# Two column groups of an output projection by Strassen: all sixteen row tiles in the seven products

## The reference

```python
h = rms_norm(x, norm_g)                            # x: 1 x 1024 x 2048, float32
proj = jnp.einsum('bsd,de->bse', h, w_in)
...                                                # attention of heads A, B and C
mixed = jnp.concatenate([
    out_a.astype(h.dtype) * jax.nn.silu(az),
    out_b.astype(h.dtype) * jax.nn.silu(bz),
    out_c.astype(h.dtype) * jax.nn.silu(cz)], axis=-1)
return x + jnp.einsum('bse,ed->bsd', mixed, w_out) # w_out: 2048 x 2048
```

## Time and profile before

| | |
|---|---|
| time, median of 3 runs | 2041.82 us (2039.94 to 2045.06) |
| the profiled execution's own time | 2044.43 us |
| its span | 2042.7 us |
| PE busy over the span | 98% |
| DVE, ACT, POOL busy | 55%, 44%, 25% |
| from 1985 to 2018 us: PE, DVE, POOL busy of 33 us | 32.85, 33.00, 30.01 |
| granted PE clock of that stretch | 1.00 of full speed (2.4 GHz) |

### The profile page before, as it was taken

One profiled execution on the slowest core, in us unless ns is written; L12 is line 12 of the kernel. 1 busy time (PEld: TensorE's weight loads), 2 busy tenths in 40 slices (PEclk: granted clock), 3 DMA queues, 4 the chain that ended last, 5 costly groups with the idle time before them and its releaser, 6 DMA issues.

```text
span 2042.7 us, 28729 instructions
## 1 busy us (share of the span) xinstructions
PE 2008.2 (98%) x10024; PEld 1690.6 (83%) x10024; DVE 1121.9 (55%) x1733; ACT 891.1 (44%) x1504; POOL 503.1 (25%) x400
## 2 busy tenths in 40 slices
PE   6999999999999999999999999999999999999998
PEld 5788888888888888888888888888888887788787
DVE  7611456465445555555555555555555657613797
ACT  7311343444454445445454445445444556411242
POOL 0000343251531212222221212222122210002565
PEclk9999999999999999999999999999999999999999
DMA  7322424324332222222222222323232274466646
GB/s 236 81 72 71 116 68 109 100 82 103 94 98 78 61 85 78 87 67 72 87 72 85 64 89 79 107 58 98 83 97 71 85 249 145 134 200 222 237 155 196
DMA packets 204559, 223.20 MB, mean 109 GB/s; under 512 B 17336, under 2 KB 143336, under 8 KB 203328
## 3 DMA queue, kind: packets, MB, share of 16 engines
q1 hardware_dynamic: 187760, 191.73, 31.8%
q10 hardware_dynamic: 16720, 30.45, 4.0%
HBM read 173.35 MB, written 48.78 MB: 109 GB/s over the span
## 4 chain that ended last, share of the span: by engine, by line
PE 85%; DVE 7%; ACT 2%; DMA 2%; issue 2%; POOL 1%; SPq 0%; DVEq 0%; ACTq 0%; POOLq 0%
PE acc L2266 19%; PE acc L2268 19%; PE acc L2267 19%; PE pv L2504 4%; PE turned L2489 4%; PE scores L2481 2%; PE scores L2478 2%; DVE w_lo L1724 1%; DVE act_lo L2209 1%; DMA w_raw<-in_w_in_dram 1%; PE acc L2616 1%; DVE fast_out L2222 1%; PE acc L2553 1%; PE acc L2555 1%; PE acc L2554 1%
## 5 line engine op out<-in xcount | busy, mean ns | idle before, releaser
L2266 PE MATMUL acc<-act_hi,w_hi 128*128 128x512 f32 x1848 | 737.1, 399 | 2.5 <-DVE w_lo L1724 1.9
L2268 PE MATMUL acc<-act_hi,w_lo 128*128 128x512 f32 x1848 | 722.0, 391 | 0.0
L2267 PE MATMUL acc<-act_lo,w_hi 128*128 128x512 f32 x1848 | 720.7, 390 | 0.0
L2268 PEld LDWEIGHTS acc<-act_hi,w_lo 128*128 128x128 f32 x1848 | 346.9, 188 | 75.4
L2266 PEld LDWEIGHTS acc<-act_hi,w_hi 128*128 128x128 f32 x1848 | 347.5, 188 | 69.5 <-DVE w_lo L1724 4.8
L2267 PEld LDWEIGHTS acc<-act_lo,w_hi 128*128 128x128 f32 x1848 | 347.7, 188 | 65.2
L1724 DVE TENSOR_TENSOR w_lo<-w_raw,w_hi 128x512 fp32r<-128x512 f32 x223 | 199.4, 894 | 358.6 <-ACT w_hi L1239 358.3
L1545 ACT ACTIVATE prob<-prob,neg_max 128x128 f32<-128x128 f32 (+7 forms) x160 | 124.0, 775 | 251.1 <-DVE neg_max L2035 251.1
L1159 POOL TENSOR_TENSOR vz<-raw 32x512 f32<-32x512 f32 x72 | 85.6, 1189 | 468.3 <-ACT sq L1492 465.6
L1239 ACT ACTIVATE w_hi<-w_raw 128x512 fp32r<-128x512 f32 x223 | 139.1, 624 | 137.2 <-PE acc L2268 110.1
L2051 DVE TENSOR_TENSOR pt_lo<-turned,pt_hi 128x1024 fp32r<-128x1024 f32 (+1 forms) x120 | 114.9, 957 | 146.9 <-ACT pt_hi L1553 146.3
(11 more groups left out here) (427 smaller groups left out, 3007.0 us busy)
## 6 DMA issues: line engine op xcount, KB each, us to landing
w_raw<-in_w_in_dram SPq DMA_DIRECT2D x240, 256.0 KB, 2.9
proj_scratch<-stage ACTq DMA_DIRECT2D x116, 256.0 KB, 2.1
w_raw<-in_w_out_dram SPq DMA_DIRECT2D x64, 256.0 KB, 3.5
raw<-proj_scratch SPq DMA_DIRECT2D x20, 512.0 KB, 3.4
logit_bias<-in_w_out_dram SPq DMA_DIRECT2D x35, 256.0 KB, 4.6
act_lo<-mixed_scratch SPq DMA_DIRECT2D x7, 1024.0 KB, 8.6
t_raw<-in_w_out_dram SPq DMA_DIRECT2D x28, 256.0 KB, 3.7
extra_raw<-in_w_out_dram SPq DMA_DIRECT2D x23, 256.0 KB, 3.5
```

The source lines that it names most:

```text
L2266: pe.matmul(acc, hi, xh, start=first, stop=False)
L2267: pe.matmul(acc, hi, xl, start=False, stop=False)
L2268: mm = pe.matmul(acc, lo, xh, start=False, stop=end)
```

## The change

Left runs 0 and 1 are gone. `FAST_ROWS` now has eight row tiles in each set, tile 9 last of the second, so that a product has eight items of 12 matmuls. Left run 2 (tile 9 for group 0) moves ahead of product 0. The order is: item 0 (left run 2), product 0 (items 1 to 8), product 1 (9 to 16), and so on to product 6 (49 to 56). The row sums, 40 instead of 35, stand at steps 6 to 45 instead of 9 to 43. The eight merges of a product are spread over six steps instead of four. Two stores are new: tiles 8 and 9 of `mixed` go to DRAM, since the row sums load them again from there. Residuals and partial sums change places among `res` and `fast_out`.

```diff
-FAST_ROWS = (list(range(7)), [7] + list(range(LAST + 1, KT)))
-FAST_LEFT = (LAST - 1, LAST)
+FAST_ROWS = (list(range(LAST - 1)), [LAST - 1] + list(range(LAST + 1, KT)) + [LAST])
...
-FAST_RUNS = [("product", 0), ("product", 1), ("left", 0), ("left", 1), ("left", 2)] + [("product", q) for q in range(2, 7)]
-LEFT_ROWS = (FAST_LEFT, FAST_LEFT, FAST_LEFT[1:])
-LEFT_COLS = (FAST_CGS[0] * HALF, FAST_CGS[1] * HALF, 0)
+FAST_RUNS = [("left", 2)] + [("product", q) for q in range(7)]
+LEFT_ROWS = {2: (LAST,)}
+LEFT_COLS = {2: 0}
...
+MERGE_STEPS = 6
...
-ROW_SUM_STEP = [first + j for first in (9, 16, 23, 30, 37) for j in range(FAST_K)]
+ROW_SUM_STEP = [first + j for first in (6, 14, 22, 30, 38) for j in range(FAST_K)]
...
         elif e < n:
-            out += own[2 * (n - e - 1):2 * (n - e)]
+            out += [own[i] for i in range(len(own)) if e + 1 + i * MERGE_STEPS // len(own) == n]
...
-        merged_into = [fast_out[0], fast_out[1], res]
+        merged_into = [res, fast_out[1], fast_out[0]]
...
                 load_early_rows(n)
+                if n == 7:
+                    store_pair(LAST - 1)
                 if n == 10:
                     sp.wait_ge(mix_lo, mixed_by(KK_GATED, 1))
+                    sp.wait_ge(mixed_saved, 16 * LAST)
                     load_gate(LAST, last_column)
...
             def load_partial(t):
+                sp.dma_start(fast_out[0][:, t, :], partial[t * P:(t + 1) * P, :]).then_inc(x_in[0], 16)
+
+            def load_first_residual(t):
+                cols = slice(FAST_CGS[0] * HALF, (FAST_CGS[0] + 1) * HALF)
                 sp.wait_ge(out_saved[t], 32)
-                sp.dma_start(res[:, t, :], partial[t * P:(t + 1) * P, :]).then_inc(res_in[t], 16)
+                sp.dma_start(res[:, t, :], x_rows[t * P:(t + 1) * P, cols]).then_inc(res_in[t], 16)
...
                 k = FAST_ROWS[kh][j]
-                sp.wait_ge(quarter_done, 3 * (GROUPS + AHEAD) + EARLY - len(ROUNDS) + OUT_ORDER.index(k) + 1)
+                if k == LAST:
+                    sp.wait_ge(out_ready, 2 * NT)
+                else:
+                    sp.wait_ge(quarter_done, 3 * (GROUPS + AHEAD) + EARLY - len(ROUNDS) + OUT_ORDER.index(k) + 1)
...
             for kk in range(3, 6):
                 load_out_quarter(1, kk)
+            sp.wait_ge(o_done, LAST + 3)
+            sp.dma_start(mixed[LAST * P:(LAST + 1) * P, :], vz[:]).then_inc(mixed_saved, 16)
             sp.wait_ge(mix_lo, MIX_ALL)
+            sp.wait_ge(mixed_saved, 16 * PAIRS)
             load_res(1)
...
+            load_rows_again(1, 1, 7)
             for n in range(8, FAST_ITEMS):
                 load_terms(n)
...
-                if 28 <= n < 32:
-                    for t in range(2 * (n - 28), 2 * (n - 28) + 2):
+                if 20 <= n < 24:
+                    for t in range(2 * (n - 20), 2 * (n - 20) + 2):
                         save_merged(2, t)
-                if 45 <= n < 49:
-                    save_merged(0, 4 + n - 45)
+                if 48 <= n < 52:
+                    save_merged(0, 4 + n - 48)
```

More of the change, by code:

```diff
@@ L960, in save_out, with load_fast_residual @@
                 sp.dma_start(out_rows[t * P:(t + 1) * P, HALF:2 * HALF], res[:, t, :]).then_inc(out_saved[t], 16)
-            def load_fast_residual(c, t):
-                cols = slice(FAST_CGS[c] * HALF, (FAST_CGS[c] + 1) * HALF)
-                sp.dma_start(fast_out[c][:, t, :], x_rows[t * P:(t + 1) * P, cols]).then_inc(x_in[c], 16)
+            def load_fast_residual(t):
+                cols = slice(FAST_CGS[1] * HALF, (FAST_CGS[1] + 1) * HALF)
+                sp.dma_start(fast_out[1][:, t, :], x_rows[t * P:(t + 1) * P, cols]).then_inc(x_in[1], 16)
             def load_partial(t):
+                sp.dma_start(fast_out[0][:, t, :], partial[t * P:(t + 1) * P, :]).then_inc(x_in[0], 16)
+            def load_first_residual(t):
+                cols = slice(FAST_CGS[0] * HALF, (FAST_CGS[0] + 1) * HALF)
                 sp.wait_ge(out_saved[t], 32)
-                sp.dma_start(res[:, t, :], partial[t * P:(t + 1) * P, :]).then_inc(res_in[t], 16)
+                sp.dma_start(res[:, t, :], x_rows[t * P:(t + 1) * P, cols]).then_inc(res_in[t], 16)
             def load_rows_again(th, kh, j):
                 k = FAST_ROWS[kh][j]
-                sp.wait_ge(quarter_done, 3 * (GROUPS + AHEAD) + EARLY - len(ROUNDS) + OUT_ORDER.index(k) + 1)
+                if k == LAST:
+                    sp.wait_ge(out_ready, 2 * NT)
+                else:
+                    sp.wait_ge(quarter_done, 3 * (GROUPS + AHEAD) + EARLY - len(ROUNDS) + OUT_ORDER.index(k) + 1)
                 sp.dma_start(raw_rows(th, kh, j), mixed[k * P:(k + 1) * P, th * HALF:(th + 1) * HALF])\
@@ L1015, in _ @@
                         for t in range(2 * (kk - 8), 2 * (kk - 8) + 2):
-                            load_fast_residual(1, t)
+                            load_fast_residual(t)
                 else:
+                    if kk == 12:
+                        load_rows_again(0, 0, FAST_K - 1)
                     load_rows_again(1, 1, kk - 12)
                     for t in range(2 * (kk - 12), 2 * (kk - 12) + 2):
-                        load_fast_residual(0, t)
+                        load_partial(t)
             load_terms(2)
@@ L1038, in _ @@
                     for t in range(2 * (n - 14), 2 * (n - 14) + 2):
-                        load_partial(t)
+                        load_first_residual(t)
                 if 18 <= n < 18 + FAST_K:
                     load_rows_again(0, 1, n - 18)
-                if 28 <= n < 32:
-                    for t in range(2 * (n - 28), 2 * (n - 28) + 2):
+                if 20 <= n < 24:
+                    for t in range(2 * (n - 20), 2 * (n - 20) + 2):
                         save_merged(2, t)
-                if 45 <= n < 49:
-                    save_merged(0, 4 + n - 45)
+                if 48 <= n < 52:
+                    save_merged(0, 4 + n - 48)
             for t in range(4):
@@ L2213, in merge @@
                 r, b, c, t, op = MERGES[i]
-                if c == 2:
+                if merged_before(i) is None and c == 0:
                     dve.wait_ge(res_in[t], 48)
                 elif merged_before(i) is None:
-                    dve.wait_ge(x_in[c], 16 * (NT // X_BUFS + NT))
+                    dve.wait_ge(x_in[c % 2], 16 * (NT // X_BUFS + NT))
                 if merged_before(i) is not None:
```

## The result

The changed kernel takes 2044.61 us (median of 21 runs, 2042.19 to 2046.55). The kernel before took 2040.84 us in 21 runs on the same chip. The ratio is 1.0017, 95% interval 1.0011 to 1.0023: 3.8 us slower, within the 0.3% that I had called no change, but clear of the noise. The profiled execution took 2044.33 us.

A forecast was written before the change was run, and what follows sets the result against it. PE was taken to bound the Strassen part. Terms -2.75 - 1.8 + 4.7 + 0.5 gave +0.65 us on a median of 2041.82, so 2042.5 us, no change within 0.3%; range 2037.3 to 2049.

The forecast's parts named there:

- A: Rival: steps with both POOL sums do no harm, only the gains stay, -4.55 us, 2037.3 us; chance 0.17.
- C: Rival: stores cost +1.3 us at early loads and item 1 waits 1 us; 2044.8 us; chance 0.08.
- the waits for splits: Sign: PE waits for splits at items 16 to 24, pieces 0.5 to 3 us, sum 3 to 6; some at 45 to 50.
- Matmuls: Strassen part on PE: 684 matmuls become 672, 12 fewer, -2.75 us.
- Waits for merges: PE's two waits of 0.86 and 0.89 us at left runs go, -1.8 us, up to -2.2 with slow restart.
- First stretch: Steps 6 to 20: DVE and POOL outlast PE's items and weights land late; PE waits +4.7 us (3.3 to 6.1).
- turns: DVE's splits and POOL's sums exclude each other, making steps 3.50 us against PE's 2.75; 3.3 us of waiting in steps 6 to 20.
- Second stretch: Steps 37 to 45, nine instead of eight long steps, after 6.0 us of regained slack: +0.5 us (0 to +2.9).
- heavy steps: Steps where POOL has both a weight sum and a row sum: 3.50 us, 0.75 more than PE's item.
- Merges, stores, SP's queue: Merges over six steps and two new stores in SP's queue: hidden, nothing; early store up to +1.3 us if not.
- The sum: Whole kernel: -2.75 - 1.8 + 4.7 + 0.5 = +0.65 us, which is no change.
- B: Rival: DMA becomes the bound from item 8 to 25; 2047.6 us if weights land in 10 us; chance 0.17.

The follow-up runs named there:

- experiment 9: Changed kernel, row sums still on POOL, with transfers spread: group 1 outputs and residuals one per item, group 0 outputs at items 28 to 31; 2041.17 us.
- experiment 5: Kernel before with only the two new stores of mixed (tiles 8 and 9) and their waits added; 2040.62 us, ratio 1.0002 to the kernel before.
- experiment 6: Changed kernel with a product's eight merges bunched in four steps instead of six; 2045.12 us, ratio 1.0021 to the kernel before.
- experiment 1: Changed kernel with POOL summing only 16 of 512 columns of each row sum, work left out; 2035.68 us, ratio 0.9976 to the kernel before.
- experiment 8: Changed kernel with row sums on DVE and the same transfers spread over more or later items, nothing left out; 2034.83 us, ratio 0.9974 to the kernel before.
- experiment 3: Changed kernel with sixteen reloads of mixed rows cut to 16 of 512 columns; 2043.41 us, ratio 1.0011 to the kernel before.
- experiment 4: Changed kernel with all forty row sums made by DVE instead of POOL, at the same steps; 2040.93 us, ratio 1.0003 to the kernel before.
- experiment 7: Changed kernel with row sums on DVE and reloads of two of four quarters of mixed cut to 16 of 512 columns; 2037.38 us, ratio 0.9985.
- experiment 2: Changed kernel with DVE making the remainder of only 16 of 512 columns of each row sum; 2036.25 us, ratio 0.9978 to the kernel before.
- experiment 10: Kernel before with its row sums moved from POOL to DVE and nothing of the change; 2041.52 us, ratio 1.0008 to the kernel before.

## Why the prediction was right, and where its sizes were off

The forecast of no change held, and so did the two sides of the account: gains of about 5 us from matmuls and merge waits, eaten by PE waiting for splits. That the time came out within 0.3% shows little, since rivals A and C would have done that too; what tells them apart is the waits for splits. They came as forecast, 3.2 us at items 19 to 26 and 1.2 at 47 to 49, though each was 0.33 to 0.48 us and not 0.5 to 3. Measured by the prediction's own steps:

- **Matmuls, -2.75.** Held. Where nothing waits an item still takes 2.75 us, and the version without any loss lasted 158.82 us: 164.26 - 2.79 - 2.75 = 158.72.
- **Waits for merges, -1.8 (up to -2.2).** Right; from start to start the two had cost 1.11 and 1.14 us, so -2.25. They stood at items 16 and 18, the first of left runs 1 and 2, and not of 0 and 1 as I had read; both went all the same. Item 1 begins 5.51 us after item 0, at 1876.27: the merges of left run 2 are hidden, as I had costed them.
- **First stretch, +4.7 (3.3 to 6.1).** Right mechanism and right bounds, size off by 1.15: 5.85 us. Taken apart by experiment 9 it is 3.9 of turns, against my 3.3, and 1.9 of late transfers, against 1.4 that the middle held. The two parts add up to nearly my upper bound of 6.1; they hardly overlapped. I had let the heavy pace end with step 20, and it ran on to the split of item 26, which is step 23. POOL was behind by then, and its row sums (two of them in a row as late as 1941.28 and 1944.78 us) still took turns with DVE. On the other side the loss per heavy item was 0.65 to 0.75.
- **Second stretch, +0.5 (0 to +2.9).** This is the step that failed in size: 2.30 us were lost against 0.54 before, +1.8. I had assumed 6.0 us of slack at its start. The slack rose only from 1.7 us at item 27 to 4.7 at item 39, 0.25 us an item, near my lower figure of 0.23: nearly every light step has a merge or two, and since DVE has no gap there, that a merge can stand beside a POOL sum brought nothing. The heavy steps themselves were sized right: they took 4.6 us of slack and 2.3 of loss, 6.9 against my 6.75. (By its own numbers the upper end of this range was 6.75 - 3.7 - 0.3 = +2.75, not +2.9.)
- **Merges, stores, SP's queue, nothing.** Held: experiments 5 and 6.
- **The sum.** -2.75 - 2.25 + 5.85 + 1.76 = +2.6, the part's measured +2.70; I had +0.65. The medians differ by 3.8. About 1 us of it lies outside what I can place: the Strassen part starts anywhere from 1869.3 to 1870.8 us in the profiles of versions that are the same up to there, and the profile of before was 3.6 us above its median, with a start at 1872.56. Its one wait for `pt_lo`, ahead of the part, was 2.8 us, where the others have 1.0 to 1.6, and its granted clock from 1600 to 1700 us was 0.98, where theirs was 1.00. What makes those differences stays open.

**The rivals.** A, that the heavy steps do no harm, is refuted for this kernel: they harm in both stretches. Its price was near for a kernel without turns: it gave 2037.3, and experiments 1 and 8 came to 2035.7 and 2034.8. B, that DMA becomes the bound, is refuted as stated by experiments 1 and 3. Two weaker forms of it hold: the order of the transfers cost 1.9 us, and with the turns gone transfers are the next bound (experiments 4, 7 and 8). Also, 396 GB/s was too high a capacity to reckon with: in the same 15 us the changed kernel moved 346 and experiment 9 moved 368 GB/s. Not all of that is capacity, since their DMA engines were not full in the first two us; from 1887 to 1900 us the kernel before moved 399, the changed one 371 and experiment 9 383. The Trainium skill ("DMA: Bandwidth & Descriptors", Where 436 GB/s comes from) puts the HBM side at about 358, and says beside it that one 16 MB transfer was measured at 425. The traces of 1887 to 1900 us lie between the two: 358 was no ceiling here. C, the stores, is refuted by experiment 5, in the kernel before; in the changed one PE waited no longer between 1640 us and the part (4.0 us, against 5.6 before), and item 1 began without a wait.

The Trainium skill ("SBUF — State Buffer", Who interferes with whom) has a rule for the turns: a DVE instruction with two SBUF inputs contends with a GpSimd instruction that reads SBUF, and one with at most one SBUF input, outside the 2-port perf modes, does not. The traces agree on both halves. Splits, with two, take 1.78 us beside a POOL sum and 0.68 alone; merges, one input of which is in PSUM, take 1.27 us for two beside a POOL sum, and 1.27 with POOL idle too (in experiment 10). Experiments 1 and 2 show that either side can be shortened to end it.

## What to carry to other kernels

When two engines stretch each other's instructions, their busy shares say little: lay both timelines side by side, take the period of the pair, and set it against the bound engine's period; the difference, times the steps in a row, less the slack, is the loss. Slack spent in one such stretch must be earned back before the next, so count what the steps between them really return. And when a change of order loses by this, try moving one partner's work to the other engine and spreading the transfers in the same edit: alone, each got back 2 to 4 us here; together, 9.8. The same move in the kernel before gained nothing, so look first at what the bound engine waits for.

## What the runs showed of the hardware

- The same sum of rows is cheaper on the busier engine. On POOL it took 1.29 us alone and 1.74 in turns, and made DVE's split beside it 1.1 us longer (1.78 for 0.68). On DVE in experiment 8 it took 0.68 us with POOL idle, and 1.78 beside one of POOL's sums of weights.
- A pause of PE that the trace shows as 0.33 to 0.47 us costs 0.65 to 0.75 us from start to start, at full clock.
- With DMA all but full, the throughput differed between kernels with other mixes and orders of transfers: 371, 383 and 399 GB/s from 1887 to 1900 us. What in the mix does it was not tested.
